# Experts 60 and 61 written back by ScalarE with plain transfers, and the gathered rows added ahead of the kept sums

## The reference

```
h = rmsnorm(x, norm_ffn)
grp = argmax(softmax(h @ w_group + b_group))             # 1 of 8 groups
top_p, top_i = top_k(softmax(expert logits of grp), 2)   # 2 of its 8 experts
weights = g_w * top_p / sum(top_p)
for each block of rows xb of expert e:                   # 64 experts
    ys = (silu(xb @ w_gate[e]) * (xb @ w_up[e])) @ w_down[e]
x = x + sum over a token's two experts of weight * its row of ys
```

## Time and profile before

| | us |
|---|---|
| median of 3 runs | 1634.4 (1633.19 to 1635.37) |
| the profiled execution, whole | 1634.71 |
| its span, first to last instruction | 1632.9 |
| TensorE busy | 1441.9 (88% of the span) |
| VectorE busy | 605.4 (37%) |
| ScalarE busy | 340.8 (21%) |
| GpSimd busy | 246.4 (15%) |

### The profile page before, as it was taken

The page is one execution under the profiler, slowest core; times in us unless marked ns, Lnnn a source line. Parts: engine busy times, 40 slices in busy tenths (PEclk is TensorE's granted clock), DMA queues, the critical chain, the costliest instruction groups (busy, mean ns, idle before and its releaser), DMA issues.

```text
span 1632.9 us, 24139 instructions
## 1 busy us (share of the span) xinstructions
PE 1441.9 (88%) x8971; PEld 900.0 (55%) x8971; DVE 605.4 (37%) x1517; ACT 340.8 (21%) x983; POOL 246.4 (15%) x290
## 2 busy tenths in 40 slices
PE   8999999999899988778778999999899977878785
PEld 3655466655466655455555555655566655555453
DVE  2245677742532222221213557423522222222225
ACT  2122377741110000000001345412100000000000
POOL 1122100000211111111112233000211111111112
PEclk9999999999899999999999999999999999999998
DMA  7115040035689999999999502473899999999997
GB/s 299 41 52 219 40 156 1 1 133 229 240 325 424 429 429 428 430 430 429 429 430 422 212 1 80 178 296 116 333 388 427 428 429 429 428 430 430 429 429 297
DMA packets 44373, 480.67 MB, mean 294 GB/s; under 512 B 11034, under 2 KB 11562, under 8 KB 24656
## 3 DMA queue, kind: packets, MB, share of 16 engines
q1 hardware_dynamic: 28144, 450.17, 65.9%
q0 software_dynamic: 15008, 25.37, 4.4%
q10 hardware_dynamic: 1152, 4.19, 0.6%
HBM read 461.33 MB, written 47.19 MB: 311 GB/s over the span
## 4 chain that ended last, share of the span: by engine, by line
PE 57%; DMA 33%; DVE 6%; issue 2%; ACT 1%; POOL 0%; DVEq 0%; SPq 0%
DMA sb_arena<-moe_w 32%; PE ps L1173 13%; PE ps L1367 7%; PE ps L1582 7%; PE ps L1182 6%; PE ps L1688 2%; PE ps L1718 2%; PE ps L1703 2%; PE ps L1548 2%; PE ps L1408 2%; PE ps L1436 2%; PE ps L1432 1%; PE ps L1519 1%; PE ps L1616 1%; PE ps L1489 1%
## 5 line engine op out<-in xcount | busy, mean ns | idle before, releaser
L1173 PE MATMUL ps<-sb_arena,sb_x_block 128*64 128x256 f32 x4096 | 478.1, 386 | 95.2 <-DMA sb_arena<-moe_w 88.6
L1173 PEld LDWEIGHTS ps<-sb_arena,sb_x_block 128*64 128x64 f32 x4096 | 420.1, 198 | 205.7 <-issue 136.0
L1182 PE MATMUL ps<-sb_arena,sb_hidden_space 128*64 128x512 f32 x1024 | 247.9, 605 | 44.1 <-ACT sb_hidden_space L898 43.7
L768 POOL DMA_INDIRECT expert_rows<-sb_y_sb,sb_row_now x124 | 132.6, 1069 | 751.6 <-DVE sb_y_sb L1954 646.3
L1953 DVE COPY sb_row_now<-sb_row_of 128x1 uint32 (+1 forms) x124 | 19.1, 154 | 599.5 <-PE ps L1182 593.2
L898 ACT COPY sb_hidden_space<-ps 128x128 f32<-128x128 f32 x128 | 34.1, 267 | 755.6 <-PE ps L1248 755.6
L1182 PEld LDWEIGHTS ps<-sb_arena,sb_hidden_space 128*64 128x64 f32 x1024 | 62.1, 136 | 141.2 <-issue 73.7
L1367 PE MATMUL ps<-sb_sorted_rows,sb_arena 128*128 128x512 f32 x256 | 114.6, 594 | 2.1 <-DVE sb_arena L2198 1.3
L1964 DVE TENSOR_TENSOR sb_x_block<-sb_sorted_rows,sb_moe_gain 128x512 f32<-128x512 f32 x124 | 85.9, 693 | 25.1 <-issue 20.7
L1954 DVE COPY sb_y_sb<-ps 128x512 f32<-128x512 f32 x124 | 84.4, 681 | 0.0
L1367 PEld LDWEIGHTS ps<-sb_sorted_rows,sb_arena 128*128 128x128 f32 x256 | 46.9, 190 | 51.4 <-issue 48.8
(11 more groups left out here) (308 smaller groups left out, 1490.0 us busy)
## 6 DMA issues: line engine op xcount, KB each, us to landing
sb_arena<-moe_w SPq DMA_DIRECT2D x116, 3072.0 KB, 38.1
sb_arena<-moe_w SPq DMA_DIRECT2D x10, 2048.0 KB, 10.1
sb_arena<-moe_w SPq DMA_DIRECT2D x16, 1024.0 KB, 6.9
sb_sorted_rows<-nsa_w_group SPq DMA_DIRECT2D x2, 2048.0 KB, 13.1
sb_arena<-nsa_w_group SPq DMA_DIRECT2D x2, 2048.0 KB, 8.2
sb_sorted_rows<-nsa_w_out SPq DMA_DIRECT2D x1, 4096.0 KB, 12.2
kept_rows<-sb_arena SPq DMA_DIRECT2D x8, 512.0 KB, 4.6
token_rows<-sb_arena ACTq DMA_DIRECT2D x8, 512.0 KB, 2.7
```

The costliest lines, as they stand in the source:

```text
L768: pool.indirect_dma_start(out=ys_dram.rearrange("r (j n) -> (r j) n", j=2), out_offset=bass.IndirectOffsetOnAxis(ap=row_now[:, u:u + 1], a ...
L1173: last = nc.tensor.matmul(ps[j * BLOCK:(j + 1) * BLOCK, bank, 0:2 * P].rearrange("p (g n) -> p g n", g=2), x_rows[:, :, k], weights[:, 0:2 ...
L1182: last = nc.tensor.matmul(ps[j * BLOCK:(j + 1) * BLOCK, 2, :], hidT[:, c * BLOCK:(c + 1) * BLOCK], weights[:, 2, c * D + j * 512:c * D + ( ...
```

## The change

There are four edits. First, POOL's loop of scatters ends two experts sooner (`DEALT_PAIRS` = 30, so experts 0 to 59), and ACT writes experts 60 and 61 (`DIRECT` = 60) itself, each by two plain transfers of 64 rows of 2 KB to `expert_rows`, which gets 64 rows more for it. All 64 rows are written, valid or not. Before the second expert's transfers ACT waits until the first one's have landed; the gathers wait for both (`written` at 64). Second, DVE copies the results of 60 and 61 with no row table, and makes the weights of the kept sums (`split_rows`, `spread_shares`) around those copies rather than ahead of them. Third, DVE adds gathered rows ahead of kept sums: three of them stand now ahead of expert 63's copy, and a tile is ready with `add_kept`, not with the second `add_rows`. Fourth, PE turns tile 0 ahead of the kept sums of tiles 2 and 3, not of tile 3 alone.

```diff
-        ys_dram = nc.dram_tensor("expert_rows", (ROWS, D), F32, kind="Internal").ap()
+        ys_dram = nc.dram_tensor("expert_rows", (ROWS + BLOCK, D), F32, kind="Internal").ap()
...
-        SENT_PAIRS = SENT // 2
+        DEALT_PAIRS = SENT // 2 - 1
+        DIRECT = 2 * DEALT_PAIRS
...
+                sp.dma_start(ys_dram[ROWS:ROWS + BLOCK, :], a["x"][0:BLOCK, :]).then_inc(rows_filled, 16)
...
-                with pool.Fori(0, SENT_PAIRS) as i:
+                with pool.Fori(0, DEALT_PAIRS) as i:
...
+                pool.wait_ge(ex[l]["written"], 64)
...
+                s = ex[l]
+                for u in range(2):
+                    gate(base + DIRECT + u, u)
+                    turn_hidden(base + DIRECT + u)
+                    row = act.value_load(start_i[0:1, l, DIRECT + u:DIRECT + u + 1], min_val=0, max_val=ROWS)
+                    act.wait_ge(y_ready, l * SENT + DIRECT + u + 1)
+                    if u == 1:
+                        act.wait_ge(s["written"], 32)
+                    for j in range(2):
+                        act.dma_start(ys_dram[bass.ds(row, BLOCK), j * 512:(j + 1) * 512],
+                                      y_sb[j * BLOCK:(j + 1) * BLOCK, u, :]).then_inc(s["written"], 16)
                 n = act.value_load(extra_n[0:1, l:l + 1], min_val=0, max_val=MAX_EXTRA)
...
+                dve.wait_ge(silu_done, base + DIRECT + 1)
+                join_hidden(0)
+                plain_block(SENT)
+                keep_rows(DEALT_PAIRS, 0)
+                split_rows(l)
+                dve.wait_ge(silu_done, base + DIRECT + 2)
+                join_hidden(1)
+                plain_block(SENT + 1)
+                spread_shares(l, 0)
+                keep_rows(DEALT_PAIRS, 1)
+                spread_shares(l, 1)
...
                 def add_kept(t):
                     dve.wait_ge(kept_done, l * TILES + t + 1)
-                    dve.wait_ge(x_loaded[t], 16 * (l + 2))
...
                 join_hidden(1)
-                keep_here(1)
-                add_kept(0)
                 add_rows(0, 0)
                 add_rows(0, 1)
-                add_kept(1)
+                add_rows(1, 0)
+                keep_here(1)
                 if l + 1 == LAYERS:
-                    add_rows(1, 0)
                     add_rows(1, 1)
+                    add_kept(0)
+                    add_kept(1)
                     for t in range(2, TILES):
-                        add_kept(t)
                         add_rows(t, 0)
                         add_rows(t, 1)
+                        add_kept(t)
                     return
```

More of the change, by code:

```diff
@@ L762, in moe_moves @@
                 if l == 0:
-                    pool.wait_ge(rows_filled, 16 * (ROWS // S))
-                with pool.Fori(0, SENT_PAIRS) as i:
+                    pool.wait_ge(rows_filled, 16 * (ROWS // S + 1))
+                with pool.Fori(0, DEALT_PAIRS) as i:
                     for u in range(2):
@@ L916, in moe_act @@
                 chunk_half(7)
-                with act.Fori(1, SENT_PAIRS) as i:
+                with act.Fori(1, DEALT_PAIRS) as i:
                     for u in range(2):
@@ L1344, in moe_pe @@
                 kept_sums(1, 1)
-                for u in range(2):
-                    kept_sums(2, u)
                 if l + 1 < LAYERS:
                     turn_tile(x_of[1], 0)
-                for u in range(2):
-                    kept_sums(3, u)
+                for t in range(2, TILES):
+                    for u in range(2):
+                        kept_sums(t, u)
             def project_out(w, layer):
@@ L1950, in keep_rows @@
                     if l > 0 or not isinstance(i, int) or i > 0:
-                        dve.wait_ge(y_written[u], i * 16 + 16 * SENT_PAIRS * l)
-                    nc.vector.tensor_copy(row_now[:, u:u + 1], row_of[:, bass.ds(i * 2 + u, 1)])
+                        dve.wait_ge(y_written[u], i * 16 + 16 * DEALT_PAIRS * l)
+                    if not isinstance(i, int) or i < DEALT_PAIRS:
+                        nc.vector.tensor_copy(row_now[:, u:u + 1], row_of[:, bass.ds(i * 2 + u, 1)])
                     nc.vector.tensor_copy(y_sb[:, u, :], ps[:, 2, :]).then_inc(y_ready, 1)
@@ L2000, in moe_dve @@
                 keep_rows(0, 1)
-                with dve.Fori(1, SENT_PAIRS - 1) as i:
+                with dve.Fori(1, DEALT_PAIRS - 1) as i:
                     for u in range(2):
@@ L2008, in moe_dve, with plain_block @@
                         keep_rows(i, u)
+                def plain_block(n):
+                    r = dve.value_load(start_i[0:1, l, n:n + 1], min_val=0, max_val=ROWS)
+                    take_block(r, n % 2).then_inc(block_ready, 1)
                 for u in range(2):
-                    dve.wait_ge(silu_done, base + SENT - 2 + u + 1)
+                    dve.wait_ge(silu_done, base + DIRECT - 2 + u + 1)
                     join_hidden(u)
-                    r = dve.value_load(start_i[0:1, l, SENT + u:SENT + u + 1], min_val=0, max_val=ROWS)
-                    take_block(r, u).then_inc(block_ready, 1)
-                    if u == 0:
-                        split_rows(l)
-                    spread_shares(l, u)
-                    keep_rows(SENT_PAIRS - 1, u)
+                    plain_block(DIRECT + u)
+                    keep_rows(DEALT_PAIRS - 1, u)
+                dve.wait_ge(silu_done, base + DIRECT + 1)
[9 more added lines that the diff above has]
+                spread_shares(l, 1)
                 s = ex[l]
@@ L2021, in moe_dve @@
                     for u in range(2):
-                        dve.wait_ge(y_written[u], 16 * SENT_PAIRS * (l + 1))
+                        dve.wait_ge(y_written[u], 16 * DEALT_PAIRS * (l + 1))
+                    dve.wait_ge(s["written"], 64)
                     dve.wait_ge(extra_made, 16 * 2 * (l + 1))
@@ L2080, in moe_dve @@
                 turns[0] += 1
+                add_rows(1, 1)
                 turned_half(m, 0)
-                add_rows(1, 0)
-                add_rows(1, 1)
-                add_kept(2)
+                add_kept(1)
                 add_rows(2, 0)
                 add_rows(2, 1)
+                add_kept(2)
                 turned_half(m, 1)
-                add_kept(3)
                 add_rows(3, 0)
                 add_rows(3, 1)
+                add_kept(3)
             def add_output(layer):
```

22 lines of the change are left out of this document (11 added, 11 removed).

## The result

| | before | after |
|---|---|---|
| median of 4 runs each, us | 1634.88 (1633.19 to 1637.25) | 1650.41 (1648.60 to 1651.21) |
| ratio, 95% interval | | 1.0101 (1.0087 to 1.0115) |
| span of the profiled execution, us | 1632.9 | 1649.4 |

The change makes the kernel 15.5 us slower. The forecast was 1644.4: the direction and the mechanism held, the size was 6 us short. The time lies at the upper edge of the forecast's own range (1638 to 1650) and inside the whole one (1632 to 1656).

The account below looks back on a forecast made before the run. Weights pace the expert stages; at their ends PE bounds layer 0 and DVE layer 1. Losses of 7.6, 0.5 and 1.9 make 10.0: 1634.7 + 10.0 - 0.3 = 1644.4 us, own range 1638 to 1650, whole 1632 to 1656.

Parts of the forecast that it names:

- Part 1: Layer 0: expert 60's write lands at 889.1, ACT waits for it, gate 62 comes at 890.4, 3.1 us later.
- The one-packet-a-turn rule: Beside the weights, an engine serves one small packet per large one, about 1 us a turn in layer 0.
- The rival of fast writes: Several packets go per turn, so layer 0's gathers start at 890: 1636.2 us in all, chance 0.22.
- the one in line behind SyncE: ACT's transfers cannot pass SP's deep queue, so gates come 17 and 10 us late: 1657 us, chance 0.13.
- Part 2: Layer 0: expert 61's write goes out at 889.2, lands at 896, gathers start at 897 instead of 893.67.
- My 1.3 us of start: Time added to each plain write before its packet turns, taken from 512 KB ACT transfers on an idle engine.
- my ten turns of 1 us: Layer 0, expert 60's write: ten packets on each DMA engine, about 1 us a turn beside weights, 10 us.
- Part 3: Three adds ahead of expert 63's copy wait for the third gather: 7.6 us lost in layer 0, 0.5 in layer 1.
- its formula (11.6 for the third): Layer 0: gathers landing evenly spread put the third 11.6 us after the first issue; the forecast took 9.5.
- Part 4: PE's waits drop its clock to half: 1.9 us taken, between bounds 0 and 4.0.

Follow-up runs that it names:

- e9: The kernel after, but ScalarE does gate 62 and its copy of the turned hidden rows before it waits and sends expert 61: ratio 1.0096.
- e3: The kernel before, scatters kept, with only the new order of adds on VectorE and of kept sums and turn on TensorE: 1642.02 us, ratio 1.0043.
- e12: The kernel before with tile 0 turned ahead of tiles 2 and 3's kept sums, and three unread products in TensorE's idle time before it: ratio 1.0016.
- e11: The kernel after with each plain write's first half of columns sent by ScalarE and the second half by POOL: ratio 1.0072.
- e1: The kernel after, but expert 61 is sent without waiting for expert 60's write, to a tensor of its own: 1643.53 us, ratio 1.0051.
- e4: The kernel before with only tile 0's turn moved ahead of the kept sums of tiles 2 and 3: 1638.10 us, ratio 1.0019.

## Why the prediction was right, and where it was short

**Part 1, the first write and ScalarE's wait: right, though 2 to 3 us short.** Predicted was a landing at 889.1, gate 62 at 890.4. On before's clock (after's gate 61 is 0.55 later) it landed at 890.9, and gate 62 came at 893.5, since two issues and the checks behind them took 2.5 us and not 1.3. By e9 these 3 us at the gate were hidden. The one-packet-a-turn rule that I took from POOL's queue holds for ScalarE's (46 beside 50). The Trainium skill's rule in "DMA: Bandwidth & Descriptors", section "Queues, rings and completion order", that an engine drains a packet of typically 9 to 17 descriptors before it changes queue, could have let all of one transfer's go at once. In this case's rows 46 packets beside 50 are about three of each on an engine; had all five of a transfer gone in one turn, two turns would have moved all 160, and the first write took 13 us and not the rival's 3 to 4. The rival of fast writes is out, and so is the one in line behind SyncE: q10 moves while q1 still has packets.

**Part 2, when the gathers start: the step that failed.** It had 897, the trace has 902.3 on before's clock, 5.3 later. 1.9 of that is the later issue of the second write, 891.1 for 889.2. The rest is its length: I gave it 6.8 from issue to landing, and it took from 891.64 to 901.91, 10.3. My 1.3 us of start came from transfers on an idle engine. Here the first packet moved more than 3 us after the issue, so the start was the term mis-sized. In the first write most of this was hidden, by luck, in my ten turns of 1 us, which were too many: from 888 us on q1 moves 4 KB packets (321 with 1.29 MB until 891.5), so the last turns were short. In layer 1 the second write took 5.3 us, where I had 3.8, and the first had landed 0.9 later than I had it, so the gathers are 2.3 late there too (1610.6 on before's clock for 1608.3).

**Part 3, the adds ahead of the copy: right, with a better reason than mine.** From the first gather's issue to the third add it took 8.9 us, I had 9.5. From the copy to the mixer's start it was 9.2, of which I had 8.2 and the clock the rest. But I had not seen how far the halves cover each other. If the writes had been as fast as the scatters, the order alone would still have cost 8.4 us in layer 0 (e3): gathers that start early land late, while the next mixer's weights are moving. By its formula (11.6 for the third) my own numbers said so, and I used them only for a rival.

**Part 4, the clock: right in kind, half in size.** 1.9 us was taken in all. I had TensorE stand only ahead of the kept sums; that it would also stand 5.7 us for the held gate, and the clock fall there first, I had not seen. The stretches of after at half clock:

```profile
895.00:899.00 4.00, 3.64 (x11) 1.03 (x12) 0.00 (x0) 1.18 (x2) 0.00 (x0) 0.50 0.96 405
...
914.00:918.00 4.00, 4.00 (x11) 1.47 (x12) 2.04 (x2) 0.00 (x0) 0.09 (x1) 0.53 1.03 403
```

The first one (down of 62, 3.68 us instead of 1.94) is hidden by the gathers, as e9 shows. The second costs 1.0, and nothing in layer 1, where VectorE is the bound.

Together: layer 0 has 7.6 of the sum, + 4.7 (the copy at 912.55 on before's clock, not 907.8), + 1.0 of clock = 13.3, measured 13.4. Layer 1 has 0.5 + 2.6 (the copy at 1620.9, not 1618.3) - 0.2 = 2.9. 8.1 and 1.9 were predicted, 16.3 measured.

What stays open: what the DMA engines do in the 3 us before the first packet and what sets their length (the last section shows that it is not the size of the packets beside it; nothing else was tried), and whether e12's gain in the trace is there in the times.

## What to carry to other kernels

A small transfer on a second queue isn't small beside a stream of large packets: count its start (here more than 3 us) and, while the stream's packets are large, one of them for each of its own on an engine, and if a second one has to wait for it, count it twice in series. Before work is moved ahead of a copy that another engine waits for, look at when its data land under the load of the moment, and not how long a transfer takes when nothing else moves. An engine's idle time is worth filling only where that engine sets the end: with late writes the same new order gave back 5.1 us in layer 1 and cost 5.5 in layer 0.

## What I had not expected of the hardware

- While q1 is at work a transfer's first packet moved more than 3 us after its issue at the end of layer 0 (no packet of q10 from 879 to 882, nor from 892 to 895). The size of q1's packets does not explain it. In the first stretch they had mostly 24 KB, in the second mostly 4 KB (219 with 1.32 MB). In e11, whose second write goes out at 886.75 (first half) and 887.26, q1 had the engines to itself from 887.3 to 890 us, all with 4 KB:

```profile
q1 hardware_dynamic: 275, 1.11, 102.0%
```

- In layer 1, where q1 is nearly through (0.2 MB from 1620 to 1622), the start was shorter: the second write of after goes out at 1617.98, and 30 packets had moved by 1620 (the two queues from 1618 to 1620):

```profile
q1 hardware_dynamic: 196, 0.71, 86.7%
q10 hardware_dynamic: 30, 0.05, 10.3%
```

- The first gather of 128 rows of 4 KB could be added 9.1 us after its issue (e1) or 8.2 (e3) while q1 moved 2.17 and 1.68 MB, and 4.3 us after it when q1 was through (the kernel after). Against e1, a start 8.3 us later cost 3.5 us in the landing.
- The clock fell to 1.2 GHz after 3.58 us in which TensorE did nothing (e4), and not after 1.72 (before) or 0.76 (e12); the 16 records of kept sums after it needed 5.73 us for 3.70.
